# Sparse-attention heads of both key groups stacked in pairs on 128 partitions

## The chip, the cores and the metric

The kernel runs on one NeuronCore of one Trainium2 chip. The metric is the device time of one execution in microseconds; the number that is compared is the median of several executions. The time before is 1242.42 us (median of 3 runs, 1241.47 to 1244.25).

## What is computed

A two-layer decoder trunk on 256 positions with 1024 channels, in float32. Layer 0 is the one that is touched: an input projection whose columns feed eight sparse-attention heads (head width 64, two key groups of four heads each, three branches: compressed blocks, selected blocks, window) and eight forgetting-attention heads; then an output projection and a dense SwiGLU. Layer 1 is gated linear attention and a mixture of eight experts. The part that matters here, cut from the reference:

```python
qg = qa[block].reshape(B, Q_BLOCK, G, R, dh)            # G = 2 key groups, R = 4 heads in each, dh = 64
s_c = einsum('bqgrd,bngd->bgrqn', qg, k_cmp) * scale    # 15 compressed blocks
p_c = masked_softmax(s_c, cmp_end <= tq)
s_s = einsum('bqgrd,bgqkd->bgrqk', qs, kg) * scale      # selected blocks (with 4 blocks all are selected)
s_w = einsum('bqgrd,bkgd->bgrqk', qg, kw) * scale       # window of 512, which covers all 256 positions
s_f = einsum('bqhd,bkhd->bhqk', q, kb) * scale + cq[..., None] - cum_t[:, :, None, :]   # forgetting heads
```

So both the selected and the window branch are plain causal attention over 256 keys, eight heads each, with their own keys.

## The kernel before, in words

Each engine has its program written out by hand, and semaphores order them. Positions are two tiles of 128 (`t` = 0, 1). Weights stream from memory in units of 1 MB through a ring of eight buffers (`raw`); ScalarE (ACT) makes a rounded copy (`whi`, `split`), VectorE (DVE) the remainder (`low`), and TensorE (PE) makes each product in three matmuls (`mm3`, lines 559 to 561). The input projection of layer 0 has six groups of columns, `in_group(0)` to `in_group(5)`, 48 matmuls of 512 columns each but for the narrower group 1.

Between these groups, and inside them by hooks, PE does the small work of the attention:

- line 678: after `in_group(2)` it transposes the four sparse keys (two branches, two key groups) of each tile, 64 columns at a time, into banks 0 and 1; DVE copies them to `keyT` (line 1710).
- lines 697 to 711: `queries_turned(i)` transposes four query heads, 64 columns at a time, and ACT copies them to `qT` (`queries_copied`, line 1253). Calls 0 and 1 stand ahead of `in_group(5)`, calls 2 and 3 are a hook at its block 2 (`later_queries`).
- line 732: the hook `block_scores` at block 4 of `in_group(5)` makes the running sum of the forget gates (lines 725 to 727, semaphore `cum`), then 16 products of one head with the 15 compressed keys of its group, and then, behind a wait for `aug`, the first sixteen transposes of the forgetting heads (`fox_turned`, line 718). `aug` is given by DVE (line 1773) once it has `cum`.
- after `in_group(5)` come sixteen more transposes, two of the block probabilities (line 751), and the attention loop.

The attention loop has 18 units, each with 512 score columns: for each of three branches (selected, window, forgetting) two units of four heads for tile 0 (128 keys) and four units of two heads for tile 1 (256 keys). For a unit `u` PE makes the scores (`qk`, line 772) and adds the mask with one bfloat16 matmul (line 774), DVE takes the row maxima (lines 1813, 1814), ACT the exponentials with their sums (line 1325), PE transposes the probabilities (`turn`, line 784), DVE copies them (line 1842), and PE multiplies by the values (`pv`, line 802). PE's order is `qk(u+2)`, `turn(u)`, `pv(u-1)`. DVE's order is the maxima of `u+2`, the copy of `u`, and after the last unit of a sequence (a branch and tile) four operations that scale and add its output (`take`, lines 1821 to 1828). Scores rotate over three banks (0, 1, 6). The queries and keys of the first two branches stand on partitions 0 to 63, with two rows of zeros below them, so that all score matmuls read 66 partitions. A float32 matmul is two records on PE in this trace, a transpose one.

Of the kernel before, what the change touches and what calls it, by code (L numbers as in the profile page):

```python
# [151 lines left out]
def trunk(nc, x_d, w_d, const_d, mask_d, small_d, comp_d, wa2_d, row_d, out_d):  # L152
    ctx = ExitStack()
    with ctx:
# [60 lines left out]
        qT = c0(NH * SEQ).rearrange("p (h n) -> p h n", h=NH)  # L215
        keyT = c0(4 * SEQ).rearrange("p (h n) -> p h n", h=4)
# [164 lines left out]
        for br in range(3):  # L381
            for t in range(NT):
                n = 4 if t == 0 else 2
                att_units += [(br, t, h0, n) for h0 in range(0, NH, n)]
        AU = len(att_units)

        def seq_of(u):
            return att_units[u][0] * NT + att_units[u][1]

# [100 lines left out]
        def _(pool):  # L490
# [19 lines left out]
            link(nc.gpsimd.memset(qT[HD:66, :, :], 0.0))  # L510
            link(nc.gpsimd.memset(keyT[HD:66, :, :], 0.0))
# [42 lines left out]
        def _(pe):  # L554
# [121 lines left out]
            for t in range(NT):  # L676
                for kk in range(4):
                    last = nc.tensor.transpose(bank[t][0:HD, kk * P:(kk + 1) * P],
                                               proj[0][:, t, 256 + kk * HD:256 + (kk + 1) * HD], ident)
                last.then_inc(S["headT_psum"], 1)  # L680
# [15 lines left out]
            nc.tensor.transpose(bank[3][0:HD, 256:286], kcm[0:30, 3, :], ident[0:30, 0:30]).then_inc(S["kcmpT_psum"], 1)  # L696
            def queries_turned(i):

                t, half = i // 2, i % 2
                for j in range(4):  # L700
                    h = half * 4 + j
                    last = nc.tensor.transpose(bank[i][0:HD, j * P:(j + 1) * P],
                                               proj[2][:, t, h * HD:(h + 1) * HD], ident)
                last.then_inc(S["headT_psum"], 1)

            def later_queries():

                pe.wait_ge(S["vbd"], 1)
                pe.wait_ge(S["kcmpT"], 1)
                queries_turned(2)  # L710
                queries_turned(3)
# [9 lines left out]
            def block_scores():  # L721
# [6 lines left out]
                pe.wait_ge(S["headT"], 6)  # L728
                for t in range(NT):
                    for h in range(NH):  # L730
                        g = h // 4
                        last = mm(bank[4][:, t * P + h * 16:t * P + h * 16 + NCMP], qT[0:HD, h, t * P:(t + 1) * P],  # L732
                                  kcmpT[0:HD, g * NCMP:(g + 1) * NCMP], start=True, stop=True)
                last.then_inc(S["cmp_s"], 1)
# [1581 lines left out]
```

## Time and profile before

| | |
|---|---|
| median of 3 runs | 1242.42 us |
| lowest, highest | 1241.47, 1244.25 us |
| the profiled execution: its own time | 1243.23 us |
| its span in the profile | 1241.3 us |
| granted TensorE clock, mean | 0.996 of full speed |
| PE busy | 1225.8 us (99%) |
| DVE busy | 982.0 us (79%) |
| ACT busy | 817.5 us (66%) |
| the attention loop, first score matmul to the output projection | 94.34 to 139.24 us of the span |

The profile gives each record of an engine a start and a duration. A matmul's duration overlaps its neighbours' (its end is modelled), so what a matmul costs is the step from its start to the next start, and a row that merges `x8` records costs the step from its start to the start of the next row.

### The profile page before, as it was taken

What the parts mean: (1) busy time and instruction counts of PE and PEld (TensorE: products, weight loads), DVE (VectorE), ACT (ScalarE), POOL (GpSimd) and SP (SyncE); (2) the same over time, 40 slices, a digit from 0 to 9 for tenths busy, and PEclk for the clock granted to TensorE, in tenths of its full rate; (3) what the DMA queues carried; (4) which work ended last, traced back from release to release, by engine and by line L of the source; (5) the groups of instructions that cost most, each with busy time, mean ns of one, the idle gap of its engine ahead of it and who ended that gap; (6) DMA issues with size and microseconds to landing.
All of it is one profiled execution on the core that took longest, in us unless ns stands there. A gap on an engine that the chain in (4) does not pass through costs nothing.

```text
span 1241.3 us, 16187 instructions
## 1 busy us (share of the span) xinstructions
PE 1225.8 (99%) x6021; PEld 1020.5 (82%) x6021; DVE 982.0 (79%) x966; ACT 817.5 (66%) x891; POOL 36.1 (3%) x42
## 2 busy tenths in 40 slices
PE   8999999999999999999999999999999999999998
PEld 6889888888889886888888888888888888888886
DVE  5978664554567558999889889889889989989896
ACT  7745364344376547777777777777777777777774
POOL 1000000000000001000000000000000000000200
PEclk9989999999999999999999999999999999999999
DMA  9731135554444345999999999999999999999992
GB/s 355 291 107 35 61 143 204 204 190 174 171 178 145 128 153 195 362 395 362 407 373 382 401 373 374 399 380 370 397 381 370 397 381 367 391 372 367 397 422 93
DMA packets 53000, 361.42 MB, mean 291 GB/s; under 512 B 6048, under 2 KB 6560, under 8 KB 10944
## 3 DMA queue, kind: packets, MB, share of 16 engines
q1 hardware_dynamic: 49872, 349.41, 72.9%
q0 software_dynamic: 3056, 11.02, 2.3%
q8 instruction: 50, 0.82, 0.3%
q14 instruction: 22, 0.18, 0.0%
HBM read 354.63 MB, written 5.77 MB: 290 GB/s over the span
## 4 chain that ended last, share of the span: by engine, by line
PE 96%; DVE 1%; ACT 1%; DMA 1%; issue 0%; SPq 0%; DVEq 0%
PE bank L559 28%; PE bank L561 28%; PE bank L560 28%; PE bank L1101 2%; PE bank L772 1%; PE bank L802 1%; PE bank L960 1%; DMA raw<-in_weights 1%; PE bank L784 1%; PE bank L569 1%; PE bank L1066 0%; PE bank L718 0%; PE bank L848 0%; DVE low L1564 0%; PE bank L732 0%
## 5 line engine op out<-in xcount | busy, mean ns | idle before, releaser
L2151 DVE TENSOR_TENSOR low<-raw,whi 128x2048 fp32r<-128x2048 f32 x260 | 594.9, 2291 | 66.4 <-ACT whi L1498 59.2
L1498 ACT CAST whi<-raw 128x2048 fp32r<-128x2048 f32 x260 | 497.3, 1913 | 114.4 <-PE bank L561 113.8
L559 PE MATMUL bank<-whi,hT_hi 128*128 128x512 f32 (+1 forms) x1104 | 431.2, 391 | 1.4 <-DVE low L1564 0.9
L561 PE MATMUL bank<-whi,hT_lo 128*128 128x512 f32 (+1 forms) x1104 | 429.0, 389 | 0.0
L560 PE MATMUL bank<-low,hT_hi 128*128 128x512 f32 (+1 forms) x1104 | 428.3, 388 | 0.0
L559 PEld LDWEIGHTS bank<-whi,hT_hi 128*128 128x128 f32 x1104 | 207.6, 188 | 44.6 <-issue 1.5
L561 PEld LDWEIGHTS bank<-whi,hT_lo 128*128 128x128 f32 x1104 | 207.4, 188 | 42.9
L560 PEld LDWEIGHTS bank<-low,hT_hi 128*128 128x128 f32 x1104 | 207.6, 188 | 41.7
L1564 DVE TENSOR_TENSOR low<-raw,whi 128x2048 fp32r<-128x2048 f32 x67 | 153.1, 2289 | 45.1 <-ACT whi L1192 45.0
L559 PE MATMUL bank<-whi,h_hi 128*128 128x512 f32 x440 | 181.1, 412 | 0.0
L561 PE MATMUL bank<-whi,h_lo 128*128 128x512 f32 x440 | 172.5, 392 | 0.0
L560 PE MATMUL bank<-low,h_hi 128*128 128x512 f32 x440 | 172.0, 391 | 0.0
L1192 ACT CAST whi<-raw 128x2048 fp32r<-128x2048 f32 x67 | 127.9, 1916 | 9.8 <-PE bank L561 7.4
L561 PEld LDWEIGHTS bank<-whi,h_lo 128*128 128x128 f32 x440 | 82.6, 188 | 17.9
L560 PEld LDWEIGHTS bank<-low,h_hi 128*128 128x128 f32 x440 | 83.1, 189 | 14.3
L559 PEld LDWEIGHTS bank<-whi,h_hi 128*128 128x128 f32 x440 | 82.7, 188 | 13.7
L1515 ACT ACTIVATE sg<-bank 128x256 f32<-128x256 f32 x88 | 33.9, 385 | 65.2 <-PE bank L561 65.2
L1348 ACT ACTIVATE sg<-bank,rstd 128x256 f32<-128x256 f32 x22 | 10.4, 473 | 98.4 <-PE bank L561 98.4
L1870 DVE SCALAR_TENSOR_TENSOR hact<-bank,rstd,sg 128x256 f32<-128x256 f32 x22 | 10.6, 484 | 57.7 <-ACT sg L1348 57.7
L1207 ACT ACTIVATE hT_hi<-bank,sml 128x128 fp32r<-128x128 f32 x80 | 22.2, 378 | 29.7 <-PE bank L569 29.7
L2156 DVE TENSOR_TENSOR h_lo<-bank,h_hi 128x256 fp32r<-128x256 f32 x88 | 36.8, 418 | 1.0 <-ACT h_hi L1502 1.0
L2168 DVE TENSOR_TENSOR hact<-sg,bank 128x256 f32<-128x256 f32 x88 | 36.5, 415 | 0.0
(313 smaller groups left out, 825.2 us busy)
## 6 DMA issues: line engine op xcount, KB each, us to landing
raw<-in_weights SPq DMA_DIRECT2D x327, 1024.0 KB, 6.1
sums<-ybuf POOLq DMA_DIRECT2D x7, 512.0 KB, 8.5
arena<-in_compress SPq DMA_DIRECT2D x1, 1088.0 KB, 15.5
x<-in_x SPq DMA_DIRECT2D x2, 512.0 KB, 5.7
raw<-in_weights SPq DMA_DIRECT2D x4, 256.0 KB, 5.7
raw<-in_weights SPq DMA_DIRECT2D x2, 512.0 KB, 9.0
tokens<-hng POOLq DMA_DIRECT2D x2, 512.0 KB, 3.6
out<-x SPq DMA_DIRECT2D x4, 256.0 KB, 3.0
```

The lines of the kernel that those rows point to most:

```text
L559: mm(out_, a_hi, b_hi, start=start, stop=False)
L560: mm(out_, a_hi, b_lo, start=False, stop=False)
L561: return mm(out_, a_lo, b_hi, start=False, stop=stop)
L1101: last = nc.tensor.transpose(bank[2][:, j * P:(j + 1) * P], hact[:, (par + c) % 2, j * P:(j + 1) * P], ident)
L1192: nc.scalar.copy(whi[:, u % SPLIT, :, :], raw[:, u % RAW, :, :]).then_inc(S["w_hi"], 1)
L1207: A(hT_hi[:, k, cols], src[:, j * P:(j + 1) * P], ACT.Copy, scale=sml[:, gc:gc + 1])\
L1498: nc.scalar.copy(whi[:, u % SPLIT, :, :], raw[:, u % RAW, :, :]).then_inc(S["w_hi"], 1)
L1515: A(sg[:, (par + c) % 2, :], bank[(par + c) % 2][:, 0:CH], ACT.Silu).then_inc(S["m_silu"], 1)
L1564: V.tensor_tensor(low[:, u % RAW, :, :], raw[:, u % RAW, :, :], whi[:, u % SPLIT, :, :].bitcast(F32), ALU.subtract).then_inc(S["w_lo"], 1)
L2151: V.tensor_tensor(low[:, u % RAW, :, :], raw[:, u % RAW, :, :], whi[:, u % SPLIT, :, :].bitcast(F32), ALU.subtract).then_inc(S["w_lo"], 1)
L2156: V.tensor_tensor(h2_lo[:, (par + c) % 2, :], bank[2][:, 0:CH], h2_hi[:, (par + c) % 2, :].bitcast(F32), ALU.subtract).then_inc(S["m_h2T"], 1)
L2168: V.tensor_tensor(hact[:, (par + c) % 2, :], sg[:, (par + c) % 2, :], bank[(par + c) % 2][:, CH:2 * CH], ALU.mult).then_inc(S["m_hact"], 1)
```

## The change

Each pair of a head of key group 0 and the head of the same rank of key group 1 now stands on one column block: group 0 on partitions 0 to 63, group 1 on 64 to 127. The query columns of the projection are reordered on the host for that. Query and key transposes take 128 columns at a time (8 and 4 in place of 16 and 8). The compressed keys are laid out block-diagonally (`kcmpT`, cleared once by GpSimd, filled by two copies), so one matmul of 30 columns gives a pair's block scores. The score matmuls of the first two branches read 64 partitions each, alternately the upper and the lower half; the scores of a pair of units are made together (`qk_pair`) and rotate over two pairs of banks, (0, 1) and (6, 7). The hook at block 2 is gone. One transpose target of the output projection's input moves from banks 0, 1 to 6, 7.

```diff
-        qT = c0(NH * SEQ).rearrange("p (h n) -> p h n", h=NH)
-        keyT = c0(4 * SEQ).rearrange("p (h n) -> p h n", h=4)
+        qT = c0(4 * SEQ).rearrange("p (r n) -> p r n", r=4)
+        keyT = c0(2 * SEQ).rearrange("p (b n) -> p b n", b=2)
...
-                att_units += [(br, t, h0, n) for h0 in range(0, NH, n)]
+                att_units += [(br, t, h0 + 4 * g, n) for h0 in range(0, 4, n) for g in range(NG)]
...
+        def score_bank(u):
+
+            return bank[SCORE_BANKS[u // 2 % 2][u % 2]]
...
-            link(nc.gpsimd.memset(qT[HD:66, :, :], 0.0))
-            link(nc.gpsimd.memset(keyT[HD:66, :, :], 0.0))
+            link(nc.gpsimd.memset(kcmpT[:, :], 0.0))
...
-                for kk in range(4):
-                    last = nc.tensor.transpose(bank[t][0:HD, kk * P:(kk + 1) * P],
-                                               proj[0][:, t, 256 + kk * HD:256 + (kk + 1) * HD], ident)
+                for br in range(2):
+                    last = nc.tensor.transpose(bank[t][:, br * P:(br + 1) * P],
+                                               proj[0][:, t, 256 + br * P:256 + (br + 1) * P], ident)
...
-            nc.tensor.transpose(bank[3][0:HD, 256:286], kcm[0:30, 3, :], ident[0:30, 0:30]).then_inc(S["kcmpT_psum"], 1)
-            def queries_turned(i):
-
-                t, half = i // 2, i % 2
-                for j in range(4):
-                    h = half * 4 + j
-                    last = nc.tensor.transpose(bank[i][0:HD, j * P:(j + 1) * P],
-                                               proj[2][:, t, h * HD:(h + 1) * HD], ident)
+            nc.tensor.transpose(bank[3][:, 256:286], kcm[0:30, 2:4, :].rearrange("p w d -> p (w d)"), ident[0:30, 0:30]).then_inc(S["kcmpT_psum"], 1)
+            def queries_turned(t):
+
+                for r in range(4):
+                    last = nc.tensor.transpose(bank[t][:, r * P:(r + 1) * P], proj[2][:, t, r * P:(r + 1) * P], ident)
                 last.then_inc(S["headT_psum"], 1)
-
-            def later_queries():
-
-                pe.wait_ge(S["vbd"], 1)
-                pe.wait_ge(S["kcmpT"], 1)
-                queries_turned(2)
-                queries_turned(3)
...
-                pe.wait_ge(S["headT"], 6)
+                pe.wait_ge(S["headT"], 4)
+                pe.wait_ge(S["kcmpT"], 1)
                 for t in range(NT):
-                    for h in range(NH):
-                        g = h // 4
-                        last = mm(bank[4][:, t * P + h * 16:t * P + h * 16 + NCMP], qT[0:HD, h, t * P:(t + 1) * P],
-                                  kcmpT[0:HD, g * NCMP:(g + 1) * NCMP], start=True, stop=True)
+                    scores_of = bank[4][:, t * P:(t + 1) * P].rearrange("p (g r n) -> p r g n", g=NG, r=4)
+                    for r in range(4):
+                        last = mm(scores_of[:, r, :, :], qT[:, r, t * P:(t + 1) * P],
+                                  kcmpT[:, :].rearrange("p (g n) -> p g n", g=NG), start=True, stop=True)
                 last.then_inc(S["cmp_s"], 1)
+                pe.wait_ge(S["vbd"], 1)
...
-            in_group(5, {2: later_queries, 4: block_scores})
+            in_group(5, {4: block_scores})
...
-            def qk(u):
+            def qk_pair(u):
 
                 br, t, h0, n = att_units[u]
                 kw = (t + 1) * P
-                b = bank[SCORE_BANKS[u % 3]]
-                if u >= 3:
+                if u >= 4:
                     pe.wait_ge(S["probs"], u - 2)
-                elif u < 2:
-                    pe.wait_ge(S["foxT"], 5 + u)
+                elif u == 0:
+                    pe.wait_ge(S["foxT"], 6)
                 else:
                     pe.wait_ge(S["proj"], 12)
                 for j in range(n):
-                    h = h0 + j
-                    if br < 2:
-                        q, k = qT[0:66, h, t * P:(t + 1) * P], keyT[0:66, br * 2 + h // 4, 0:kw]
-                    else:
-                        q, k = fqT[0:66, h, t * P:(t + 1) * P], fkT[0:66, h, 0:kw]
-                    mm(b[:, j * kw:(j + 1) * kw], q, k, start=(j == 0), stop=False)
-                own_keys = b[:, :].rearrange("p (h n) -> p h n", h=n)[:, :, t * P:(t + 1) * P]
-                mm(own_keys, mident, msk[:, 0:n * P].rearrange("p (h n) -> p h n", h=n), start=False, stop=True)\
-                  .then_inc(S["scores"], 1)
+                    for g in range(NG):
+                        h, rows = h0 + 4 * g + j, slice(g * HD, (g + 1) * HD)
+                        if br < 2:
+                            q, k = qT[rows, h0 + j, t * P:(t + 1) * P], keyT[rows, br, 0:kw]
+                        else:
+                            q, k = fqT[0:66, h, t * P:(t + 1) * P], fkT[0:66, h, 0:kw]
+                        mm(score_bank(u + g)[:, j * kw:(j + 1) * kw], q, k, start=(j == 0), stop=False)
+                for g in range(NG):
+                    own_keys = score_bank(u + g)[:, :].rearrange("p (h n) -> p h n", h=n)[:, :, t * P:(t + 1) * P]
+                    mm(own_keys, mident, msk[:, 0:n * P].rearrange("p (h n) -> p h n", h=n), start=False, stop=True)\
+                      .then_inc(S["scores"], 1)
...
-            pe.wait_ge(S["pool_chain"], 3)
-            qk(0)
-            qk(1)
+            qk_pair(0)
...
-                if u + 2 < AU:
-                    qk(u + 2)
+                if u % 2 == 0 and u + 2 < AU:
+                    qk_pair(u + 2)
...
-                if cg == 4:
-                    queries_copied(2)
-                    queries_copied(3)
                     head_root(3, 16)
...
-                V.tensor_copy(keyT[0:HD, :, t * P:(t + 1) * P], bank[t][0:HD, :].rearrange("p (h n) -> p h n", h=4))\
+                V.tensor_copy(keyT[:, :, t * P:(t + 1) * P], bank[t][:, 0:2 * P].rearrange("p (b n) -> p b n", b=2))\
...
-            V.tensor_tensor(kv[:, 0:16], rA[0:30, 0:16], rB[0:30, 0:16], ALU.add).then_inc(S["kcmp"], 1)
+            link(V.tensor_tensor(kv[:, 0:16], rA[0:30, 0:16], rB[0:30, 0:16], ALU.add))
+            V.tensor_copy(kcm[0:30, 2, :], kv).then_inc(S["kcmp"], 1)
...
-            V.tensor_copy(kcmpT[0:HD, 0:30], bank[3][0:HD, 256:286]).then_inc(S["kcmpT"], 1)
+            dve.wait_ge(S["pool_chain"], 2)
+            V.tensor_copy(kcmpT[0:HD, 0:NCMP], bank[3][0:HD, 256:256 + NCMP])
+            V.tensor_copy(kcmpT[HD:P, 16:16 + NCMP], bank[3][HD:P, 256 + NCMP:286]).then_inc(S["kcmpT"], 1)
...
-TURN_BANKS = {0: ((0, 1), (2, 3)), 1: ((0, 1), (2, 3)), 2: ((2, 3), (4, 5)), 3: ((0, 4), (3, 5)),
+TURN_BANKS = {0: ((0, 1), (2, 3)), 1: ((6, 7), (2, 3)), 2: ((2, 3), (4, 5)), 3: ((0, 4), (3, 5)),
...
-SCORE_BANKS = (0, 1, 6)
+SCORE_BANKS = ((0, 1), (6, 7))
```

## Rows read from the trace of the kernel before

**Rows 1.** The page: busy time by engine, then the granted TensorE clock in 40 slices.

```profile
PE 1225.8 (99%) x6021; PEld 1020.5 (82%) x6021; DVE 982.0 (79%) x966; ACT 817.5 (66%) x891; POOL 36.1 (3%) x42
...
PEclk9989999999999999999999999999999999999999
```

**Rows 2.** Windows: busy time (and records) by engine, granted clock, DMA share, GB/s.

```profile
98.20:106.50 8.30, 8.30 (x61) 7.43 (x59) 6.82 (x16) 4.41 (x20) 0.00 (x0) 1.00 0.00 0
...
520.00:1241.00 721.00, 715.20 (x3259) 589.15 (x3257) 645.90 (x468) 536.35 (x449) 22.08 (x18) 1.00 0.95 372
```

**Rows 3.** PE timeline, input projection: start, duration, line, out<-in, stationary, moving, count.

```profile
73.93 1.03 PE L702 MATMUL bank<-cst,arena 128*64 128x128 f32 x8
74.72 0.47 PE L559 MATMUL bank<-whi,hT_hi 128*128 128x512 f32 x1
...
77.57 0.28 PE L725 MATMUL bank<-arena,cst 128*128 128x8 f32 x2
...
77.93 0.37 PE L727 MATMUL bank<-arena,cst 128*128 128x8 f32 x2
78.23 4.57 PE L732 MATMUL bank<-arena 64*128 64x15 f32 x32
82.72 3.62 PE L718 MATMUL bank<-cst,arena 128*66 128x128 f32 x16
86.00 0.78 PE L559 MATMUL bank<-whi,hT_hi 128*128 128x512 f32 x1
...
92.38 1.91 PE L718 MATMUL bank<-cst,arena 128*66 128x128 f32 x16
94.12 0.38 PE L751 MATMUL bank<-cst,arena 128*128 128x128 f32 x2
```

**Rows 4.** Windows of half a microsecond, PE only: busy (records), granted clock, DMA.

```profile
80.00:80.50 0.50, 0.50 (x7) 1.00 1.04 442
80.50:81.00 0.50, 0.50 (x7) 0.94 1.12 475
81.00:81.50 0.50, 0.50 (x4) 0.50 0.93 393
...
87.50:88.00 0.50, 0.50 (x3) 0.73 0.00 0
```

**Rows 5.** DVE timeline: gate sums for `aug`, then the last copy of forgetting keys.

```profile
78.43 0.18 DVE L1773 TENSOR_SCALAR arena<-bank 128x16 f32<-128x16 f32 x1
...
93.89 1.40 DVE L1799 TENSOR_SCALAR arena<-bank,sml 66x512 f32<-66x512 f32 x2 [1.61 <-PE bank L718]
```

**Rows 6.** PE timeline of one unit of tile 1, then scores of tile 0.

```profile
101.94 1.08 PE L772 MATMUL bank<-arena 66*128 66x256 f32 x4
102.86 0.28 PE L774 MATMUL bank<-msk_bits 128*128 128x256 bf16 x1
102.98 0.60 PE L784 MATMUL bank<-cst,arena 128*128 128x128 f32 x4
103.41 1.00 PE L802 MATMUL bank<-arena 128*128 128x64 f32 x8
104.25 1.08 PE L772 MATMUL bank<-arena 66*128 66x256 f32 x4
...
106.56 1.11 PE L772 MATMUL bank<-arena 66*128 66x128 f32 x8
107.51 0.38 PE L774 MATMUL bank<-msk_bits 128*128 128x512 bf16 x1
```

**Rows 7.** DVE timeline in the loop: `take` from its reciprocal on, then one unit.

```profile
104.59 0.19 DVE L1821 RECIPROCAL arena<-arena 128x8 f32<-128x8 f32 x1
...
106.35 0.68 DVE L1813 TENSOR_REDUCE arena<-bank 128x2 f32<-128x512 f32 x1
107.07 0.17 DVE L1814 TENSOR_SCALAR arena<-arena 128x2 f32<-128x2 f32 x1
107.15 0.69 DVE L1842 COPY arena<-bank 128x512 f32<-128x512 f32 x1
```

More of the change, by code:

```diff
@@ L1251, in head_root, with queries_copied @@
                   .then_inc(S["head_sqrt"], 1)
-            def queries_copied(i):
-                t, half = i // 2, i % 2
-                act.wait_ge(S["headT_psum"], 3 + i)
-                nc.scalar.copy(qT[0:HD, half * 4:half * 4 + 4, t * P:(t + 1) * P],
-                               bank[i][0:HD, :].rearrange("p (h n) -> p h n", h=4)).then_inc(S["headT"], 1)
+            def queries_copied(t):
+                act.wait_ge(S["headT_psum"], 3 + t)
+                nc.scalar.copy(qT[:, :, t * P:(t + 1) * P], bank[t][:, :].rearrange("p (r n) -> p r n", r=4))\
+                  .then_inc(S["headT"], 1)
             def fox_copied(i):
@@ L1324, in _ @@
                 for j in range(n):
-                    last = A(pbuf[:, u % 2, j * kw:(j + 1) * kw], bank[SCORE_BANKS[u % 3]][:, j * kw:(j + 1) * kw], ACT.Exp,
+                    last = A(pbuf[:, u % 2, j * kw:(j + 1) * kw], score_bank(u)[:, j * kw:(j + 1) * kw], ACT.Exp,
                              scale=HD ** -0.5, bias=negm[:, seq_of(u), h0 + j:h0 + j + 1],
@@ L1812, in rowmax @@
                 m = negm[:, seq_of(u), h0:h0 + n]
-                link(V.tensor_reduce(m, bank[SCORE_BANKS[u % 3]][:, :].rearrange("p (h n) -> p h n", h=n), AX.X, ALU.max))
+                link(V.tensor_reduce(m, score_bank(u)[:, :].rearrange("p (h n) -> p h n", h=n), AX.X, ALU.max))
                 V.tensor_scalar(m, m, -HD ** -0.5, None, ALU.mult).then_inc(S["rowmax"], 1)
@@ L2246, in layout @@
     qa, kc, vc, ksl, vsl, kwn, vwn, ga, qb, kb, vb, fb = np.split(w, cut, axis=1)
+    qa = qa.reshape(DM, NG, 4, HD).transpose(0, 2, 1, 3).reshape(DM, NH * HD)
     first = pack_blocks(np.concatenate([kc, vc, ksl, kwn], axis=1))
```

## The prediction, made before the changed kernel was run

> **What bounds the kernel now.** I read the page first: PE is busy 99% of the span, DVE 79%, ACT 66% [rows 1]. The reader should see that no other engine comes near. The windows by stage say the same inside the attention loop: in 98.20 to 106.50 PE is busy all 8.30 us and DVE 6.82 of them [rows 2]. So time that PE saves ends the kernel earlier, if DVE and ACT keep up and nothing later takes it back. The last 721 us run with the transfers at 0.95 of their share and PE busy 715.20 us [rows 2]; PE's own pace sets them, the ring is full when they begin, and they move as a block. Then I read PE's timeline, start to next start, around each edited line, and last DVE's, since a stage in which DVE fills 6.82 of 8.30 us has little room.
>
> The clock line has an 8 in its third slice [rows 1]. The half-microsecond windows place it: 1.00 until 80.50, 0.50 (1.2 instead of 2.4 GHz) from about 80.9 to 87.7 [rows 4]. Before it fell, PE had run 15-column block-score matmuls since 78.23, and 8-column ones before those [rows 3].
>
> **Key transposes (line 678): eight become four.** Eight transposes of 64 columns step 73.93 to 74.72, 0.79 us [rows 3], 0.10 each. A transpose of 128 columns steps 102.98 to 103.41 for four, 0.11 each [rows 6]. So four fewer save 0.4 us. DVE's two copies read half as many columns; DVE is not late there, so I cost that at nothing.
>
> **Query transposes (lines 697 to 711): sixteen become eight.** The eight in the hook go: 0.79 us [rows 3]. The eight ahead of `in_group(5)` stay eight, now of 128 columns. ACT makes two copies less; the next thing it does, a square root for DVE, is then earlier than DVE asks for it. Nothing further.
>
> **Block scores (line 732): 32 records become 16.** They run 78.23 to 82.72, 4.49 us, partly at the low clock [rows 3, 4]. Seven records touch a half-microsecond window at full clock; a record shows 0.26 us, so the step is near (0.50 + 0.26) / 7 = 0.11 [rows 3, 4]. With 15 columns moving this is the load of 128 stationary columns, so 30 columns do not lengthen it. Sixteen take 1.8 us: 2.7 saved, of which 32 x 0.11 = 3.6 against 4.49 makes 0.9 clock and 1.8 work.
>
> **The clock after it.** Sixteen transposes of line 718 run 82.72 to 86.00, 3.28 us; the next sixteen 92.38 to 94.12, 1.74 [rows 3]: 1.5 lost. The second half of `in_group(5)`, 24 matmuls, runs 86.00 to 92.38, 6.38 us; twelve at full clock run 74.72 to 77.57, 2.85, so 24 should take 5.7 [rows 3]: 0.7 lost. With 0.9 above the low clock costs 3.1 us. After the change the thin matmuls start at 77.57 - 0.4 - 0.8 = 76.4 and end at 76.4 + 0.66 (lines 725 to 727, 77.57 to 78.23 [rows 3]) + 1.8 = 78.8, 2.4 us of them. In this trace the clock fell 3.3 us after 77.57, so I take it that it stays up.
>
> **What is late next.** The transposes of line 718 wait for `aug`, which DVE gave at 78.43 + 0.18 = 78.6 [rows 5]. PE used to come four microseconds later; now it comes at 78.8. DVE's row is solid before that and gains two small operations (a copy of 30 x 64 with its link, and a second `kcmpT` copy), 0.3 us by its small rows of 0.17 to 0.19 [rows 5, 7]. So `aug` comes at 78.9 and with the wait PE loses 0.2. Behind it everything up to the loop is driven by PE: the last key copy on DVE waited 1.61 us for PE [rows 5]. The softmax of the block scores starts on DVE only after its next weight unit (2.29 us), at 81.2, and is due at 88 on PE: covered.
>
> Sum ahead of the loop: 0.4 + 0.8 + 2.7 + 1.5 + 0.7 - 0.2 = 5.9 us.
>
> **The score matmuls (line 772) in two row groups.** Serial, a unit of tile 1 costs 0.92 us (four records, 101.94 to 102.86) and one of tile 0 0.95 (eight, 106.56 to 107.51) [rows 6]. 12 of 18 units change, as four pairs of tile 1 and two of tile 0. No row of this trace shows two row groups, so I bound it. Dear end: no overlap, 1.84 and 1.90 a pair. Cheap end: matmuls start in order, and each float32 matmul is two records on the same rows, so upper, upper, lower, lower, upper...: every second record can start together with its predecessor, and 8 records take 5 steps, 16 take 9. That is 1.15 and 1.07 a pair. Weight loads may still go one by one; the block scores show 0.11 for one of 64 rows [rows 3, 4]. At 0.11, 8 loads are 0.9 and hide under 1.15, but 16 loads are 1.8: no gain in tile 0. I take the nearest rows: 1.15 and 1.8.
>
> Each pair goes into the 64-row shape and out of it. The one such step in the trace is line 727 to 732: second record of 727 at 77.93 + 0.37 - 0.26 = 78.04, next start 78.23, 0.19 where 0.11 is usual, so 0.08 [rows 3]. Twelve steps: 1.0 us; below zero is excluded, nothing in it can speed PE. Dear end: 0.3 each, a whole matmul's latency. Loop on PE: 4 x 0.69 + 2 x 0.1 - 1.0 = 2.0 us saved.
>
> **The pairing puts a wait on PE.** Before, between `turn(u)` and `pv(u)` stood `pv(u-1)`, scores and mask of a unit, and `turn(u+1)`: 0.84 + 1.04 + 0.43 = 2.3 us [rows 6]. Now for even `u` no scores stand there: 1.27 us. In it DVE has to finish the maxima of `u+2` (0.80) and the copy of `u` (0.69) [rows 7], which start when the pair's first mask ends; with 0.3 for two handovers that is 1.8 against mask 0.12 + 0.43 + 1.27 = 1.8 on PE. Just even, and late where `take` adds 104.59 to 106.35 = 1.76 us [rows 7] and at the first unit, where DVE still has the last keys, `pcT` and two outputs to do. Walking the units with these steps I find about 0.8 us at the start and 0.6 over the sequence ends. Behind the waiting `pv(u)` stands the next `qk_pair`. DVE in a branch needs 6 x 1.5 + 2 x 1.76 = 12.5 us, PE 14.1 before (four units of 2.31, 101.94 to 104.25, and two of 2.44) and 13 now [rows 6, 7], so part of any further PE saving would be lost to DVE. Loop: 2.0 - 1.4 = 0.6 saved.
>
> The other edits (GpSimd's clearing, bank rotation, the moved transpose target) lie beside idle engines or free banks: nothing.
>
> **Sum.** 5.9 + 0.6 = 6.5 us. The profiled execution took 1243.23, 0.8 above the median; it would go to 1236.7, and the median of 1242.42 to 1235.9.
>
> **The skill's pages.** The Trainium skill, TensorEngine Tiling (Array Packing), Key Properties, says that different tiles load and multiply in parallel and that a change of tiling mode drains the engine. By the first half the loads overlap as well (the fourth case below); by the second the step of 0.08 should be there each time, and the row at line 732 agrees in sign. The Trainium skill, TensorE: Matmul & The Clock Gate, Part 4, says that transposes do not count as activity for the clock. The trace speaks for it: through the sixteen transposes at 82.72 to 86.00 the clock stayed at 0.50. By that rule 1.74 us of transposes lengthen the thin stretch, which is the third case.
>
> **Rivals.**
> - Forecast (0.44): wide overlap, clock stays up: 1235.9.
> - No overlap (0.22): row groups run one after the other. Against it speaks nothing here; for it, that no row shows overlap. PE gains nothing, loses 1.0 in steps, and about 0.9 of waits: loop 1.9 slower, total 5.9 - 1.9 = 4.0: 1238.4.
> - The clock still falls (0.16): thin matmuls 76.4 to 78.9, then transposes to 80.7, 4.3 us without a 512-column matmul, against 8.4 before. Price at most the 3.1 of before; half of it, 1.6: 1237.5.
> - Loads overlap too (0.10): 9 steps in tile 0, 1.5 more saved on PE, of which DVE leaves about 1: 1234.9, and 1233.7 if the waits are not there.
> - Slower (0.05): overlapped matmuls plus the waits leave PE doing less, and in the loop's first two branches, 28 us, the clock falls to 1.2 GHz. Speaks against it: 1.00 all through the loop now, and each wait is under a microsecond. Each microsecond at half speed costs half of one; it decides from about 18 us (6.5 + 2.5 lost); all 28 us: +14, 1250.
> - The last 0.03: no overlap and low clock together, 1240.0.
>
> 0.2% is 2.5 us, about what a measurement of this kernel can tell from no change, so faster means below 1239.9. That holds for the first four cases and not for all of their spread: 0.88; same 0.07; slower 0.05. Range 1233.6 to 1239.6.
>
> **What would show it.** Line 732 with 16 records in 1.8 us; granted clock 1.00 in the slice; line 718 starting near 79.0 and its sixteen in 1.74; second half of `in_group(5)` in 5.5 to 5.7. In the loop, records of one score pair starting two at a time (1.15 us from first score to first mask, against 1.84), `pv` of even units waiting for line 1842 by tenths. Wrong if the score pair takes 1.84 or more, if the step to the mask is several tenths, or if line 718 waits for `aug` by a microsecond.

## The result, and the profile after

The changed kernel took 1234.28 us (median of 4, 1234.17 to 1234.76) beside 1241.95 for the kernel before (median of 4, 1241.02 to 1244.25): a ratio of 0.9939, 95% interval 0.9923 to 0.9955, or 7.7 us less. Forecast were 6.5 us less and 1235.9, in a range of 1233.6 to 1239.6. Two later measurements of the same kernel, beside the kernel before in the lots of the experiments, gave 1235.59, ratio 0.9950 (0.9933 to 0.9967), and 1234.76, ratio 0.9942 (0.9929 to 0.9956): 6.5 and 7.1 us less. So the gain is 6.5 to 7.7 us.

The page of the changed kernel: PE is still busy 99% of the span, with 10.2 us less busy time than in [rows 1], and no slice of the clock line is below 9.

```profile
PE 1215.6 (99%) x5993; PEld 1010.0 (82%) x5993; DVE 981.1 (80%) x968; ACT 816.8 (66%) x889; POOL 35.8 (3%) x41
...
PEclk9999999999999999999999999999999999999999
```

PE's timeline of the changed kernel ahead of the loop, with the columns of [rows 3]. From one row's start to the next is what a step costs.

```profile
75.43 0.28 PE L718 MATMUL bank<-arena,cst 128*128 128x8 f32 x2
76.01 1.95 PE L726 MATMUL bank<-arena 128*128 128x32 f32 x16
78.05 1.91 PE L711 MATMUL bank<-cst,arena 128*66 128x128 f32 x16
79.71 0.48 PE L562 MATMUL bank<-whi,hT_hi 128*128 128x512 f32 x1
...
85.28 1.91 PE L711 MATMUL bank<-cst,arena 128*66 128x128 f32 x16
...
87.33 1.16 PE L767 MATMUL bank<-arena 64*128 64x128 f32 x16
```

The block scores (now line 726) step 2.04 us where they took 4.49 [rows 3]. The row shows 32 moving columns, two groups of 16, and not the 30 of the description of the change and of the prediction: `kcmpT` is 32 columns wide, with one column of zeros for each group. The transposes behind them (711) step 1.66 instead of 3.28, and the second half of `in_group(5)` 5.57 instead of 6.38. The granted clock, in a half-microsecond window of the changed kernel with the columns of [rows 4], is 1.00 where it had begun to fall to 0.50:

```profile
80.50:81.00 0.50, 0.50 (x4) 1.00 0.00 0
```

The loop of the changed kernel, PE's timeline: the first pair of tile 1 with the start's waits, a pair of tile 0, the last pair of tile 1 with a wait behind it, and the first records after the loop. Rows of before for the same things are [rows 6]; a bracket names idle time and what ended it.

```profile
90.68 1.14 PE L767 MATMUL bank<-arena 64*128 64x256 f32 x8
91.75 0.39 PE L770 MATMUL bank<-msk_bits 128*128 128x256 bf16 x2
91.97 0.60 PE L780 MATMUL bank<-cst,arena 128*128 128x128 f32 x4
92.81 0.66 PE L780 MATMUL bank<-cst,arena 128*128 128x128 f32 x4 [0.24 <-ACT arena L1316]
93.61 1.10 PE L798 MATMUL bank<-arena 128*128 128x64 f32 x8
...
98.61 1.16 PE L767 MATMUL bank<-arena 64*128 64x128 f32 x16
99.71 0.60 PE L770 MATMUL bank<-msk_bits 128*128 128x512 bf16 x2
...
108.45 0.60 PE L780 MATMUL bank<-cst,arena 128*128 128x128 f32 x4
109.30 1.10 PE L798 MATMUL bank<-arena 128*128 128x64 f32 x8 [0.24 <-DVE arena L1836]
...
130.19 0.48 PE L562 MATMUL bank<-whi,hT_hi 128*128 128x512 f32 x1
```

Two units of tile 1 step 1.07 us from first score to first mask (90.68 to 91.75) against 2 x 0.92 in [rows 6], and two of tile 0 step 1.10 (98.61 to 99.71) against 2 x 0.95. But a transposition `turn` that steps 0.43 in [rows 6] steps 0.84 and 0.80 at the start, and 0.85 at 108.45: PE waits before the next row can start. DVE fills 6.75 of 8.00 us in this stretch, as it filled 6.82 of 8.30 in [rows 2]:

```profile
98.00:106.00 8.00, 8.00 (x74) 6.83 (x73) 6.75 (x15) 4.43 (x23) 0.00 (x0) 1.00 0.01 2
```

**Where the time went.** The profiled execution of after took 1234.34 us (span 1232.4), that of before 1243.23 (1241.3). PE's timeline splits the 8.9 us between the spans so (before less after, us):

| stretch | measured | predicted |
|---|---|---|
| start-up, until the first key transposes (46.12, 45.32) | 0.8 | 0 |
| key and query transposes | 1.3 | 1.2 |
| gate sums, then block scores with the wait for `aug` | 0.1 + 2.4 | 2.5 |
| transposes of line 718, now 711 | 1.6 | 1.5 |
| second half of `in_group(5)` | 0.8 | 0.7 |
| step to the first scores | -0.1 | 0 |
| ahead of the loop, without start-up | 6.2 | 5.9 |
| loop: 94.34 to 139.24, now 87.33 to 130.19 | 2.0 | 0.6 |
| after the loop | -0.1 | 0 |

The start-up is not the change's: key transposes begin anywhere from 45.04 to 46.12 in the profiles here, whatever the kernel; two other profiles of the changed kernel have 45.65 and 45.20, and `e5_wide_fillers`, made from the kernel before, has 45.19. Without it the timeline shows 8.1 us, and the three ratios 6.5 to 7.7.

In the loop the pairs of tile 1 gave 3.0 and those of tile 0 1.5 us (a little less than four and two times the differences above, since the first units of before step 0.87 and 0.89), the change of array shape took back 0.5, and new waits 1.9. The experiments are about these terms and about the clock.

The share of the clock differs from one execution to the next. Of the 51 executions of the kernel before that were timed beside the experiments, 15 have a mean granted clock of 0.996 and take 1242.5 us on average, 26 have 0.997 and take 1241.7, and the one with 0.999 took 1238.78. The profiled one has 0.996. Of the 13 executions of the changed kernel, nine have 0.999 (1234.4 us on average) and four 0.998 (1236.1). The span times what the mean clock lacks to 1 is 0.0033 x 1241 = 4.0 us before and 0.0013 x 1234 = 1.6 after (the clock also falls in the last microseconds of every profile). The difference, 2.4 us, is an estimate of what the clock gives on average, against the 3.1 that the profiled execution of before had lost.

### The profile page after: what moved, and what is told of

It is laid out like the page before. It is cut to its first block, busy times and chain, and to the rows that moved or that the text cites. A ratio compares the mean times of both kernels' runs of the same rounds, so it can differ in the third digit from the quotient of the medians.

```text
span 1232.4 us, 16130 instructions
## 1 busy us (share of the span) xinstructions
PE 1215.6 (99%) x5993; PEld 1010.0 (82%) x5993; DVE 981.1 (80%) x968; ACT 816.8 (66%) x889; POOL 35.8 (3%) x41
## 4 chain that ended last, share of the span: by engine, by line
PE 95%; DVE 2%; ACT 1%; DMA 1%; issue 0%; SPq 0%; DVEq 0%
PE bank L562 29%; PE bank L564 29%; PE bank L563 29%; PE bank L1095 2%; PE bank L798 1%; PE bank L954 1%; PE bank L767 1%; DMA raw<-in_weights 1%; PE bank L572 1%; PE bank L1060 0%; PE bank L780 0%; PE bank L842 0%; DVE low L1555 0%; ACT hT_hi L1201 0%; PE bank L674 0%
```

## The experiments

**First lot.** Theory: two row groups overlap because the loop alternates between them (line 760), the rest of the change in the loop (pairs, four banks) brings nothing by itself, the clock stayed up because the thin matmuls are fewer, and the waits come from DVE taking the maxima of the next pair before the copy of the running one. Each has a kernel.

`e1_rows_in_turn`: the changed kernel with the two loops of `qk_pair` swapped, so that all records of one row group come first.

```diff
-                for j in range(n):
-                    for g in range(NG):
+                for g in range(NG):
+                    for j in range(n):
```

> The changed kernel with one edit: in a pair of units all score matmuls of the upper 64 rows are issued first, then all of the lower, instead of in alternation. Theory (the row groups overlap, 1.07 to 1.10 us a pair where a serial pair took 1.84 to 1.90): 8 records then take 7 steps instead of 5, 16 take 15 instead of 9, so PE's work grows by about 4 x 0.46 + 2 x 0.6 = 3.0 us, and since part of the waits for DVE and ACT shrinks when PE is slower, the kernel gets 1.5 to 3.0 us slower: about 1236.6. Rival (the gain in the loop came from the four banks and the paired order, not from overlap): within 0.5 us of 1234.3.

Measured: 1235.45 us, ratio to before 0.9952 (0.9935 to 0.9969); the loop takes 43.59 us instead of 42.86. PE's timeline of this kernel at the start of the loop, and last the answer for a stretch of 0.03 us, 90.96 to 90.99:

```profile
87.07 1.71 PE L767 MATMUL bank<-arena 64*128 64x128 f32 x16
88.94 0.38 PE L770 MATMUL bank<-msk_bits 128*128 128x512 bf16 x1 [0.16 <-issue]
89.16 1.88 PE L805 MATMUL bank<-arena 128*128 128x512 f32 x4
90.97 1.14 PE L767 MATMUL bank<-arena 64*128 64x256 f32 x8
92.04 0.39 PE L770 MATMUL bank<-msk_bits 128*128 128x256 bf16 x2
```

```profile
90.97 0.49 PE L767 MATMUL bank<-arena 64*128 64x256 f32 x2
```

The pair of tile 1 still steps 1.07 (90.97 to 92.04) though four records of one group stand ahead of four of the other. The pair of tile 0, eight and eight, takes 2.09 us with its masks (87.07 to 89.16) instead of 1.54 (in after, to 88.87). So the order matters for 8 + 8 records and not for 4 + 4: the loss falls short of what was expected, and "matmuls start in order", on which the prediction's cheap end rests, is wrong as a rule here. In order, the first record of the lower group could start no earlier than the fourth of the upper, three steps of 0.22 after the first; but two records start within 0.03 us at 90.97, at the very beginning. In the pair of tile 0 five records start one by one (87.07 to 87.62) before the second group joins at 87.63. The median lies inside the changed kernel's three (1234.28 to 1235.59), so it is the rows and the loop's 0.7 us that carry this, not the median.

`e2_pairs_without_rows`: the kernel before, with pairs and four banks but each matmul on 66 rows as it was.

```diff
-                b = bank[SCORE_BANKS[u % 3]]
-                if u >= 3:
-                    pe.wait_ge(S["probs"], u - 2)
+                b = bank[SCORE_BANKS[u % 4]]
+                if u >= 4:
+                    pe.wait_ge(S["probs"], u // 2 * 2 - 2)
...
-                if u + 2 < AU:
+                if u % 2 == 0 and u + 2 < AU:
                     qk(u + 2)
+                    qk(u + 3)
...
-SCORE_BANKS = (0, 1, 6)
+SCORE_BANKS = (0, 1, 6, 7)
```

> The kernel before with one part of the change alone: score products of two units made together and four score banks (0, 1, 6, 7), heads still one by one on 66 rows. Theory (pairing costs: it takes the scores away from between a transposition and the values it feeds): PE's work stays, waits of 0.5 to 1.5 us appear, 1242.5 to 1243.5. Rival (the paired order or the fourth bank is what saves in the loop): 1240 to 1241.5.

Measured: 1241.94, ratio 1.0002 (0.9993 to 1.0012); loop 91.92 to 137.29 = 45.37 us, 0.5 more than before. In its timeline PE waits for DVE at the start, where before has no such wait:

```profile
99.27 0.99 PE L802 MATMUL bank<-arena 128*128 128x64 f32 x7 [0.35 <-DVE arena L1843]
```

Pairs and banks save nothing; they bring the wait at the start, and none at the sequence ends. The gain of the pairs in the loop is the row groups'. The median is below the 1242.5 to 1243.5 that was expected, and the clock is a reason: in this kernel's profile, with the same thin matmuls as before ahead of the loop, the granted clock was low from about 80.9 to 84.3 only, 3.4 us instead of 6.8.

```profile
80.50:81.00 0.50, 0.50 (x6) 0.85 0.97 410
...
84.00:84.50 0.50, 0.50 (x5) 0.73 0.00 0
```

The block scores, the transposes and the second half of `in_group(5)` took 12.5 us (77.34 to 89.88) against 14.15 in [rows 3].

`e3_copy_first`: DVE copies unit `u` before it takes the maxima of `u+2`.

```diff
-                if u + 2 < AU:
-                    rowmax(u + 2)
...
+                if u + 2 < AU:
+                    rowmax(u + 2)
```

> The changed kernel with one edit: DVE copies the transposed probabilities of unit u before it takes the maxima of unit u+2, not after. Theory (in the loop 2.0 us were saved where PE's matmuls alone became 4.7 shorter, and the rest is PE waiting for DVE's copies): 0.4 to 1.0 us faster, 1233.3 to 1233.9. Rival (the waits are for ACT's exponentials, which then start later): the same or up to 1 us slower.

Measured: 1235.80, ratio 0.9958 (0.9944 to 0.9972); loop 44.43, so 1.6 longer. The waits have moved: PE waits for ACT's exponential, which now gets its maxima late. A row of the waits in 86 to 132 (total us, times, longest):

```profile
PE bank L780 <- ACT arena L1316: 2.1, 4, 0.7
```

The theory that DVE's order makes the waits fell; either order leaves one of two consumers late.

`e4_scores_in_32_records`: the changed kernel with the block scores issued per group again, 32 records of 16 columns (on 128 rows, with the same zeros).

```diff
-                        last = mm(scores_of[:, r, :, :], qT[:, r, t * P:(t + 1) * P],
-                                  kcmpT[:, :].rearrange("p (g n) -> p g n", g=NG), start=True, stop=True)
+                        for g in range(NG):
+                            last = mm(scores_of[:, r, g, :], qT[:, r, t * P:(t + 1) * P],
+                                      kcmpT[:, g * 16:(g + 1) * 16], start=True, stop=True)
```

> The changed kernel with one edit: the block scores are made one key group at a time from the block-diagonal keys, 16 products of 16 columns and so 32 records instead of 16, all on 128 rows. Work alone is 16 x 0.11 = 1.8 us more, of which the 0.2 us wait for the gate sums goes: plus 1.6, 1235.9. Theory (the clock fell because the thin stretch was long): it falls again to 1.2 GHz and costs 1 to 3 us more, 1237 to 1239. Rival (the clock fell for the 64-row shape or for something else that is gone): clock 1.00 throughout and 1235.9.

Measured: 1238.99, ratio 0.9975 (0.9966 to 0.9985), 3.4 to 4.7 us above the changed kernel; its ten executions have mean clocks of 0.996 to 0.998. The timeline, then windows of one microsecond, PE only:

```profile
76.04 4.34 PE L727 MATMUL bank<-arena 128*128 128x16 f32 x32
80.22 3.60 PE L711 MATMUL bank<-cst,arena 128*66 128x128 f32 x16
...
90.09 1.91 PE L711 MATMUL bank<-cst,arena 128*66 128x128 f32 x16
```

```profile
78.00:79.00 1.00, 1.00 (x11) 0.98 0.97 410
79.00:80.00 1.00, 1.00 (x6) 0.50 0.89 377
```

From line 726 or 727 to the second transposes it is 14.05 us here (76.04 to 90.09) and 9.27 in after: 4.8 more. The clock has fallen to its lower level (1.2 GHz) at 79.0, which makes 3.2 of it: 32 records 4.18 where 32 x 0.11 = 3.6, transposes 3.25 (to 83.47) instead of 1.66, second half 6.62 instead of 5.57. The other 1.6 are the sixteen records. The theory held: with 32 thin records in place of 16 the clock falls, and on 128 rows as on the 64 of before, so the array's shape is not what does it.

**Second lot**, with the changed kernel once more for comparison (`a1_changed_again`: 1235.59, loop 42.84, granted clock 1.00 through it).

> The changed kernel itself, timed beside the next three on the same chip: 1234.3 us, with 1.07 us for a pair of score units of tile 1 and 1.10 (in some runs 1.3) for one of tile 0.

The "in some runs 1.3" is no slower pair: in those traces the record of the pair's first mask is missing, so the step ends at the second, 0.22 us later.

`e5_wide_fillers`: the kernel before with three groups of wide bf16 matmuls (512 columns) ahead of each tile's sixteen thin ones.

```diff
                 for t in range(NT):
+                    keep_busy(3, 3)
                     for h in range(NH):
```

> The kernel before with six idle bfloat16 matmuls of 512 columns added among the thin block-score matmuls, three ahead of each tile's sixteen; they write a free bank. They cost 6 x 0.22 = 1.3 us. Theory (the clock fell because the thin stretch was long, and cost 3.1 us in the profiled run of before): it stays at 1.00 and the kernel gets 1 to 2 us faster than before, 1240 to 1241. Rival (the clock falls for another reason, or its price is smaller than the steps said): 1.3 us slower than before, 1243.4.

Measured: 1244.22, ratio 1.0019 (1.0008 to 1.0030). Its timeline and two windows (with the columns of the last ones):

```profile
77.96 1.95 PE L733 MATMUL bank<-arena 64*128 64x15 f32 x16
...
80.60 2.63 PE L733 MATMUL bank<-arena 64*128 64x15 f32 x16
83.16 3.62 PE L718 MATMUL bank<-cst,arena 128*66 128x128 f32 x16
```

```profile
81.00:82.00 1.00, 1.00 (x9) 0.84 0.12 49
82.00:83.00 1.00, 1.00 (x6) 0.50 0.00 0
```

The clock fell all the same, in the second sixteen, though 0.8 us of wide matmuls stood ahead of them (79.84 to 80.60). The theory that such fillers hold it up fell; by their steps they cost 1.3 us (77.44 to 77.96 and 79.84 to 80.60), and the median is 2.1 up.

`e6_sixty_four_rows`: the kernel before with its score matmuls on 64 rows, so without any second row group.

```diff
-                        q, k = qT[0:66, h, t * P:(t + 1) * P], keyT[0:66, br * 2 + h // 4, 0:kw]
+                        q, k = qT[0:HD, h, t * P:(t + 1) * P], keyT[0:HD, br * 2 + h // 4, 0:kw]
```

> The kernel before with one edit: the score matmuls of the selected and window branches read 64 partitions instead of 66 (the two left out are rows of zeros); one row group, three banks, old order. The run with the rows in turn showed 1.07 us for a pair of tile 1 though it did not alternate the row groups. Theory now (a float32 matmul on 64 rows moves its columns at twice the pace of one on 66 to 128, whichever row group it is in): a unit of tile 1 goes from 0.92 to about 0.55, one of tile 0 stays near 0.95 because 128 stationary columns take 0.11 to load; 8 x 0.37 less 24 shape changes of which those at the mask cost up to 0.1: 1 to 2.5 us faster than before. Rival (only matmuls in two different row groups overlap, as the prediction had it): no gain, 0 to 1 us slower than before.

Measured: 1245.63, ratio 1.0030 (1.0018 to 1.0041), 3.5 us slower. Its timeline of one unit:

```profile
101.79 1.00 PE L802 MATMUL bank<-arena 128*128 128x64 f32 x8
102.72 1.13 PE L772 MATMUL bank<-arena 64*128 64x256 f32 x4
103.78 0.28 PE L774 MATMUL bank<-msk_bits 128*128 128x256 bf16 x1
```

Four records on 64 rows step 1.06 where 66 rows step 0.92 [rows 6], and the `pv` ahead 0.93 instead of 0.84. So one stay in the 64-row shape costs 0.14 + 0.09 = 0.23 us, and 64 rows are not faster in themselves: the rival, that only different row groups overlap, was right in kind, but its time (0 to 1 us slower) was not. Twelve stays of 0.23 make 2.8 of the 3.0 us that the loop got longer (93.93 to 141.87).

`e7_pairs_for_tile0_only`: the changed kernel, where units of tile 1 and of the forgetting branch are issued one at a time, each on its row group.

```diff
-                    for g in range(NG):
+                    for g in parts:
...
-                if u % 2 == 0 and u + 2 < AU:
-                    qk_pair(u + 2)
+                if u + 2 < AU:
+                    if att_units[u + 2][0] < 2 and att_units[u + 2][1] == 0:
+                        if u % 2 == 0:
+                            qk_pair(u + 2)
+                    else:
+                        qk_pair((u + 2) // 2 * 2, (u % 2,))
```

> The changed kernel with one edit: only the scores of tile 0 in the first two branches, where the alternation saves loads (1.10 against 1.87 us a pair), are made in pairs; all other units' scores are made one unit at a time, as before, so that they stand again between a transposition and the values it feeds. Theory (the paired order itself costs waits, 2.6 us of them in the loop): 0.5 to 1.5 us faster than the changed kernel, 1233 to 1233.8. Rival (the waits are DVE's and ACT's own pace, whatever PE's order): within 0.4 us of 1234.3, or slower by the additional shape changes, 4 x 0.1.

Measured: 1237.07, ratio 0.9964 (0.9952 to 0.9977); loop 45.57 us, 2.7 more than after. Its timeline:

```profile
106.54 1.13 PE L767 MATMUL bank<-arena 64*128 64x256 f32 x4
107.60 0.28 PE L770 MATMUL bank<-msk_bits 128*128 128x256 bf16 x1
```

PE has no waits here, which gives back 1.9 us, but a single unit of tile 1 takes 1.06, as much as a pair (1.07): eight units cost 8 x 1.06 against 4 x 1.07, 4.2 more, and four more entries into the shape about 0.4. 4.2 + 0.4 - 1.9 = 2.7. The theory that giving up the pairs of tile 1 pays fell: the overlap is worth more than the waits that it brings.

**Third lot** (`a2_changed_third`: 1234.76, loop 42.85). Open were the waits at the sequence ends and the clock.

> The changed kernel itself once more, timed beside the next three: between 1234.2 and 1235.7 us, as its two medians so far.

`e8_copy_first_even`: the copy first, but only for even units.

```diff
-                if u + 2 < AU:
+                if u + 2 < AU and u % 2:
                     rowmax(u + 2)
...
+                if u + 2 < AU and u % 2 == 0:
+                    rowmax(u + 2)
```

> The changed kernel with one edit: DVE copies before it takes the maxima for even units only (where the values of unit u follow 1.27 us behind its transposition); for odd units the maxima stay first. In the run with copies first everywhere, PE waited 2.1 us for ACT at the transpositions of odd units, whose maxima had come late. Theory (even and odd units want opposite orders): 0.3 to 0.8 us faster than the changed kernel beside it. Rival (DVE's total work sets the pace, and order only moves the wait): within 0.3 us, or slower.

Measured: 1235.62, ratio 0.9953 (0.9939 to 0.9966); loop 44.05, 1.2 more than in `a2_changed_third`. Its timeline at the sequence end:

```profile
109.75 1.10 PE L798 MATMUL bank<-arena 128*128 128x64 f32 x8 [0.80 <-DVE arena L1836]
```

Now the odd units' copies are late by 0.8. This theory fell as well: DVE's order is a choice of where PE waits.

`e9_short_take`: DVE's `take` does its two wide operations for one head of eight only.

```diff
-                link(V.tensor_tensor(heads(tmpo), o, bc(fac[:, q, :], 2, HD), ALU.mult))
-                V.tensor_tensor(oacc[:, t, 0:512], oacc[:, t, 0:512], tmpo, ALU.add).then_inc(S["o_done"], 1)
+                link(V.tensor_tensor(heads(tmpo)[:, 0:1, :], o[:, 0:1, :], bc(fac[:, q, 0:1], 2, HD), ALU.mult))
+                V.tensor_tensor(oacc[:, t, 0:HD], oacc[:, t, 0:HD], tmpo[:, 0:HD], ALU.add).then_inc(S["o_done"], 1)
```

> The changed kernel with DVE's work at the end of a sequence cut: the scaling and adding of the output (two operations of 512 columns, four times) is done for the first of eight heads only, so the other sparse heads keep only their compressed branch. That takes 4 x 2 x 0.5 = 4 us of work from DVE in the loop. Theory (part of what the overlap saves is given back in waits for DVE, 12.5 us a branch against PE's 12): PE's waits at the ends of sequences go, 0.8 to 1.5 us faster than the changed kernel. Rival (the waits are the latency of the chain maxima, exponentials, transposition, copy, whatever DVE's load): within 0.3 us of it.

Measured: 1233.57, ratio 0.9930 (0.9916 to 0.9943); loop 41.88, 0.97 less than in `a2_changed_third`. The same `turn` and `pv` in PE's timeline, first of `a2_changed_third`, then of this kernel:

```profile
108.35 0.60 PE L780 MATMUL bank<-cst,arena 128*128 128x128 f32 x4
109.19 1.10 PE L798 MATMUL bank<-arena 128*128 128x64 f32 x8 [0.24 <-DVE arena L1836]
```

```profile
108.22 0.60 PE L780 MATMUL bank<-cst,arena 128*128 128x128 f32 x4
108.66 1.00 PE L798 MATMUL bank<-arena 128*128 128x64 f32 x8
```

The `turn` steps 0.44 instead of 0.84, and no `pv` of the first two branches waits for DVE's copy at a sequence end any more. The theory held: about 1 us of what the row groups save is given back to DVE at the ends of the sequences, through `take`. The `pv` of 109.30 in after is that of unit 7, an odd one, whose transposition stands at 105.76. DVE had `take` from 105.99 on, then the maxima of unit 9, and came to the copy only after them:

```profile
108.55 0.69 DVE L1836 COPY arena<-bank 128x512 f32<-128x512 f32 x1
```

`e10_thin_stretch_halved`: the kernel before with its thin matmuls in two stretches, tile 1's block scores and the transposes two blocks later.

```diff
+                tile_scores(0)
...
+            def more_scores():
+
+                tile_scores(1).then_inc(S["cmp_s"], 1)
...
-            in_group(5, {2: later_queries, 4: block_scores})
+            in_group(5, {2: later_queries, 4: block_scores, 6: more_scores})
```

> The kernel before with one edit: the block scores of tile 1 and the transposes behind them move from the hook at block 4 to a new one at block 6 of the same column group, so that twelve matmuls of 512 columns stand between two thin stretches of about 2.5 and 1.8 us in place of one of 5.1. The work is the same. Theory (the length of the thin stretch brings the clock down, at a price of 3.1 us): granted clock 1.00 and 2.5 to 3.1 us faster than before, about 1239.2. Rival (the clock falls for another reason, such as the transposes that follow): within 0.5 us of before.

Measured: 1242.87, ratio 1.0006 (0.9997 to 1.0015). The timeline, then windows of one microsecond:

```profile
77.86 1.95 PE L735 MATMUL bank<-arena 64*128 64x15 f32 x16
...
84.13 2.07 PE L735 MATMUL bank<-arena 64*128 64x15 f32 x16
86.12 1.94 PE L718 MATMUL bank<-cst,arena 128*66 128x128 f32 x16
...
96.10 1.98 PE L818 MATMUL bank<-arena 128*128 128x512 f32 x4 [1.09 <-DVE arena L1810]
```

```profile
80.00:81.00 1.00, 1.00 (x5) 0.99 1.03 434
81.00:82.00 1.00, 1.00 (x4) 0.50 0.55 229
84.00:85.00 1.00, 1.00 (x8) 0.80 0.00 0
```

The clock fell at 81.0, when 512-column matmuls had been running again for 1.3 us, and was back at 1.00 at 84.4; the second stretch, as thin and followed by sixteen transposes, ran at 1.00 from there on (transposes 1.70). The delayed scores also made PE wait 1.09 us for DVE at 96.10. So 2.5 us of thin matmuls (77.20 to 79.74) brought the clock down here, and 2.6 (75.43 to 78.05) did not in the changed kernel. The length of the stretch does not decide it alone. Nor does one profile tell of every execution: three of this kernel's eleven have a mean clock of 0.999, as most of the changed kernel's have, and took 1241.4 to 1241.7 us; the other eight have 0.997 or 0.998.

## Why the prediction was right, and where it was not

**What bounds it: right.** PE was busy 99% before and after. After the loop, the stretch of some 1102 us took 1102.1 and 1102.2: it moved as a block.

**Transposes and block scores: right.** Predicted 1.2 and 2.5 (with 0.2 of wait for `aug`), measured 1.3 and 2.4. Sixteen records of 32 columns start every 0.11 us (76.01 to 77.69) and step 2.04 with the wait, so the 0.11 a record, read from seven records in a window, holds for 32 columns too. Sixteen records more, in `e4_scores_in_32_records`, cost 1.6 at full clock, where 16 x 0.11 = 1.8.

**The clock: outcome right, reason only in part.** The second slice at 0.8 is gone, and of the 3.1 us of low clock 1.6 and 0.8 came back behind the block scores, each within 0.1 of its term; the 0.9 is inside the 2.4 of the block scores. The reason given, that the clock falls 3.3 us after the thin matmuls begin, is contradicted: in e10 it fell with wide matmuls running. e4 shows that 32 thin records against 16 make the difference here, e5 that wide fillers between them do not prevent the fall. What the chip's clock goes by is left open. In all eight profiles with sixteen records of 32 columns it stayed up until the last 10 us of the span. The 3.1 us is the price in one execution: e2's profile lost about half of it with the same thin matmuls, and the mean clocks make it some 2.4 on average. The third case, transposes that lengthen the thin stretch until the clock falls, did not happen: 1.66 us of them behind it ran at 1.00. The row that the prediction took as speaking for the page on transposes does not: the clock stayed at 0.50 through the 512-column matmuls behind them too, until 87.7 [rows 4], so it does not tell the two kinds apart.

**The scores in two row groups: that they overlap was right, how they overlap was not, and one term was mis-sized.** Pair of tile 1: predicted 1.15, measured 1.07; 3.0 us saved in all against 2.8. That the two are so near is partly luck. The 1.15 is five steps of 0.23 with starts in order; the trace has four steps, each group going at its own pace (two records at 90.68, two at 91.00, at 91.22 and at 91.43, mask at 91.75), as long as one group alone takes in e6 (1.06), and 0.2 of the 1.07 is the change of shape at both ends. Pair of tile 0: predicted 1.8, because sixteen loads of 0.11 would go one by one; measured 1.10, so the loads of the two groups overlap too. That term was 0.2 and is 1.5 us. The case given a chance of 0.10, "loads overlap too", is the one that happened; its price, 1.5 on PE of which DVE leaves about 1, is close to what the loop showed over the forecast (2.0 against 0.6), and its 1234.9 lies between the three medians. (The 1233.7 that it gives without the waits is not what its own terms make: 5.9 + 2.0 + 1.5 from 1242.42 is 1233.0.) The choice of the nearest row was the error: line 732's loads all went to the same rows, so its 0.11 says nothing of loads to two groups. The Trainium skill, TensorEngine Tiling (Array Packing), Key Properties, which the prediction weighed against that row, agrees with this trace in both halves: different tiles load and multiply in parallel (1.10 for sixteen records with their loads), and changing the tiling mode has a price (0.1 at each entry).

**The change of shape: right in sign, half in size.** Predicted 12 steps of 0.08, 1.0 us. Measured is an entry for each of six pairs, 0.1 each on the matmuls ahead (0.84 to 0.95), 0.5 in all. For a stay without a partner e6 shows 0.23; in a pair the part inside is already in the 1.07 and 1.10.

**The waits: right that DVE is late, wrong about which unit, and size 0.5 short.** Predicted 0.8 at the start and 0.6 over the sequence ends. Measured 0.9 at the start (0.41 and 0.37 in the two `turn`, 0.09 in `pv`) and 1.0 at the ends, and e9 takes exactly the latter away. The miss comes with the former one: a faster pair of tile 0 leaves DVE less time. The prediction expected `pv` of even units to wait for line 1842 (now 1836), because no scores stand between their transposition and their values. That is so at the start (unit 0, 0.37). At the sequence ends the longest waits are those of odd units, 3 and 7 (0.17 and 0.41), behind `take` and the next maxima, and e2, which has the pairs without the faster scores, has none there. At the start the exponential on ACT, which waits for the same maxima, was late too. e3 and e8 show that neither of these two orders on DVE takes them away, e7 that giving up pairs costs more than it gives.

**Slower, and no overlap:** neither happened. The clock stayed at 1.00 through the loop.

Predicted gain 6.5; the timeline shows 6.2 + 2.0 - 0.1 = 8.1 without the start-up, and the ratios 6.5 to 7.7. That the medians differ by up to 1.6 us less than the profiled executions do is in part the clock: the profiled execution of before is one of the slower ones (1243.23, mean clock 0.996), and single executions of the kernel before differ by up to 4.5 us within one lot. What the rest is stays open.

## What to carry to other kernels

Bound a resource that no row shows from rows that use it in the same way: a duration of loads to one row group is no price for loads to two. Whoever speeds up the bounding engine by a microsecond in a stretch should walk its neighbours' next deadlines with the new, shorter time, since here half of what the row groups left after the shape changes (1.9 of 4.0 us) was lost to new waits. And pack matmuls into row groups in pairs only: on one group alone the narrower shape costs time. Where the granted clock moves within a kernel, look at the mean clock of all executions before pricing it from one profile.

## What the runs showed of the hardware that was not expected

- float32 matmuls on two groups of 64 rows take the time of one group: 8 records of 256 columns 1.07 us against 1.06 for the 4 of one group (e6), 16 of 128 columns 1.10 against 1.09 for 8 (e6), weight loads included.
- They overlap even if all four records of one group are issued first (1.07); with eight of each the order costs 0.55 us a pair. The Trainium skill, TensorE: Matmul & The Clock Gate, Part 3, has matmuls in strict order of issue; the 1.07 in `e1_rows_in_turn` is less than that order allows, and two records on 64 rows start within 0.03 us there although four of one group were issued first. The measurement decides.
- One stay in the 64-row shape without a partner costs 0.23 us, part of it (0.09) in the matmuls ahead of it.
- The granted clock fell with 512-column matmuls running for 1.3 us again, and with six wide matmuls put between thin ones. With the same thin matmuls it was low for 6.8 us in one profile (before) and 3.4 in another (e2). What decides it is not settled.
